# Reordering the opening of a one-core hybrid mLSTM and MoE layer: q in passes by kind of product, gate rows at full precision, one modulation chunk by TensorE

## What is computed

```python
shift_a, scale_a, gate_a, shift_f, scale_f, gate_f = silu(c) @ w_ada + b_ada     # 6 x 1024, for two conditions
h = rmsnorm(x, g_pre_mix) * (1.0 + scale_a) + shift_a
z = h @ w_in                        # u 512, q 512, k 512, v 512, o 512, gate_pre 16 columns
y_pool = pool_mixer(u, w_pool, pool_scale, grid)
y_ml, C, n, m = mlstm_mixer(q, k, v, o, gate_pre, b_gate, C0, n0, m0)    # two directions, 4 heads of 128
x = x + gate_a * rmsnorm(concat([y_pool, y_ml]) @ w_out, g_post_mix)
h = rmsnorm(x, g_pre_ffn) * (1.0 + scale_f) + shift_f
x = x + gate_f * rmsnorm(moe(h), g_post_ffn)    # 64 experts, top 6 in 4 of 8 groups, and a shared expert
```

## Time and profile before

| | us |
|---|---|
| median of 3 runs | 728.69 (728.23 to 728.75) |
| the profiled execution, its own time | 728.3 |
| its span, first to last instruction | 726.2 |
| mean granted TensorE clock | 0.99 of full speed |

### The profile page before, as it was taken

How to read it: one execution, slowest core, us unless ns; L and a number is a source line. 1 busy time by engine, 2 the same in 40 slices (tenths; PEclk the granted TensorE clock), 3 DMA queues, 4 the chain that set the end, 5 groups by cost and what they waited for, 6 DMA issues and landing times.

```text
span 726.2 us, 11392 instructions
## 1 busy us (share of the span) xinstructions
PE 683.2 (94%) x4205; PEld 396.8 (55%) x4205; DVE 391.9 (54%) x1003; ACT 192.0 (26%) x329; POOL 89.0 (12%) x53
## 2 busy tenths in 40 slices
PE   1789999998999999999999999999999999998993
PEld 1689888777865645544444544454445445444431
DVE  3488999695298444454444444454445437442115
ACT  3244334474272311211111111111111121130113
POOL 2445544422303000000000000000000000000000
PEclk9999999999999999999999999999999999999997
DMA  9999866625579569999999999999999999999994
GB/s 321 374 351 336 260 232 232 246 103 165 155 286 423 248 251 416 427 423 427 399 383 426 426 427 423 421 424 424 425 426 423 428 422 427 424 425 424 419 409 192
DMA packets 51012, 259.14 MB, mean 357 GB/s; under 512 B 6704, under 2 KB 9312, under 8 KB 32904
## 3 DMA queue, kind: packets, MB, share of 16 engines
q1 hardware_dynamic: 46816, 252.50, 86.2%
q0 software_dynamic: 1584, 4.90, 2.0%
q10 hardware_dynamic: 2552, 0.98, 0.5%
HBM read 254.64 MB, written 3.71 MB: 356 GB/s over the span
## 4 chain that ended last, share of the span: by engine, by line
PE 80%; DMA 8%; SPq 4%; DVE 4%; issue 2%; ACT 1%; POOL 0%; DVEq 0%; ACTq 0%
PE psum L2414 23%; PE psum L2422 11%; PE psum L2302 10%; PE psum L2386 9%; PE psum L600 5%; PE psum L601 5%; PE psum L602 5%; DMA w_gu<-in_w_expert_gu 4%; PE psum L2263 3%; DMA w_gu<-in_w_ada 2%; DMA w_dn<-in_w_expert_down 2%; PE psum L2314 2%; SPq L796 1%; PE psum L2373 1%; PE psum L2006 1%
## 5 line engine op out<-in xcount | busy, mean ns | idle before, releaser
L2414 PE MATMUL psum<-w_gu,hgT 128*32 128x512 f32 (+1 forms) x1280 | 191.4, 594 | 2.1 <-DMA w_gu<-in_w_expert_gu 2.1
L2414 PEld LDWEIGHTS psum<-w_gu,hgT 128*32 128x32 f32 (+1 forms) x1280 | 57.3, 119 | 127.8 <-issue 127.6
L1781 DVE TENSOR_TENSOR f_acc<-f_acc,psum 128x512 f32<-128x512 f32 x132 | 86.7, 684 | 43.3 <-PE psum L2386 43.3
L2422 PE MATMUL psum<-w_dn,actT 128*32 128x512 f32 (+1 forms) x640 | 98.7, 597 | 1.4 <-DMA w_dn<-in_w_expert_down 0.9
L1759 DVE SCALAR_TENSOR_TENSOR act<-sil,wsl,psum 128x256 f32<-128x256 f32 x27 | 18.4, 682 | 127.8 <-ACT sil L1115 118.5
L585 POOL TENSOR_TENSOR w_lo<-w_gu,w_hi 128x2048 fp32r<-128x2048 f32 x13 | 59.8, 4597 | 75.4 <-ACT w_hi L876 75.4
L2302 PE MATMUL psum<-onehot,h_lo 128*128 128x512 f32 (+1 forms) x168 | 66.7, 397 | 0.0
L2302 PE MATMUL psum<-onehot,h_hi 128*128 128x512 f32 (+1 forms) x168 | 65.3, 389 | 0.0
L1765 DVE TENSOR_TENSOR y_lo<-psum,y_hi 128x1024 fp32r<-128x1024 f32 x26 | 31.8, 1224 | 51.0 <-ACT y_hi L1119 51.0
L2422 PEld LDWEIGHTS psum<-w_dn,actT 128*32 128x32 f32 (+1 forms) x640 | 27.0, 119 | 58.5 <-issue 57.8
L1115 ACT ACTIVATE sil<-psum 128x256 f32<-128x256 f32 x27 | 10.4, 384 | 173.2 <-PE psum L2414 173.2
(11 more groups left out here) (322 smaller groups left out, 861.4 us busy)
## 6 DMA issues: line engine op xcount, KB each, us to landing
w_gu<-in_w_expert_gu SPq DMA_DIRECT2D x49, 2048.0 KB, 17.5
w_dn<-in_w_expert_down SPq DMA_DIRECT2D x61, 1024.0 KB, 14.9
w_gu<-in_w_expert_gu SPq DMA_DIRECT2D x27, 1024.0 KB, 16.0
w_gu<-in_w_ada SPq DMA_DIRECT2D x12, 2048.0 KB, 13.9
w_gu<-in_w_in SPq DMA_DIRECT2D x4, 2048.0 KB, 12.9
w_gu<-in_w_out SPq DMA_DIRECT2D x2, 2048.0 KB, 9.2
bc<-mod_rows POOLq DMA_DIRECT2D x6, 512.0 KB, 7.3
w_gu<-in_w_expert_gu SPq DMA_DIRECT2D x6, 512.0 KB, 20.4
```

The costliest lines, as they stand in the source:

```text
L1781: v.tensor_tensor(dst, dst, bank(5 + n), ALU.add).then_inc(f_added, 1)
L2414: ins = t.matmul(bank(target)[rows, :], column(c)[:, rows], w_gu[s][:, c, :], start=(c == 0), stop=(c == NC - 1), tile_position=(0, rows.s ...
L2422: ins = t.matmul(bank(target + n)[rows, :], actT[:, j, rows], w_dn[s][:, j, 512 * n:512 * (n + 1)], start=(j == 0), stop=(j == 1), tile_po ...
```

## The change

- **Start.** ACT takes the table of Sqrt first, squares x, and only then makes silu(c). TensorE transposes x before ada(0). Products whose result nobody reads (`keep_warm`, 128 x 512 at full precision) stand before (1) and after (3) modulation_T(0).
- **q.** z_chunk("q") becomes q_chunk: by half and by kind of product. Of the first half, the high products of heads 0 to 2, then ada(1), the w_hi x tT_lo products, ada(3), the w_lo products, with modulation_T(1) among them, and then head 3. Of the second half, all high products, all w_hi x tT_lo, all w_lo.
- **Gates.** No split. wgs holds 32 columns (16 of them zero), and each of the 12 products (four of hT for the last four row blocks, four of tT_hi and four of tT_lo for the first four) is made at full precision in one of four column tiles, into bank 3. The first four (`gates_second`) come after q's first half, the rest (`gates_first`) right behind. ACT copies bank 3 to gate_part; a product with gate_sum, made of ident on DVE, adds the four tiles into bank 6 (`gates`). tT_lo of the last four row blocks, which overwrites hT, now waits for gates_second.
- **a4.** Is multiplied directly by TensorE (ada(4)) after q, and loaded behind k instead of ahead of it. DVE's sums and the total of a4 are gone.
- **Order.** DVE's gate chain comes right after tT_lo; sums of a5 come after g_nat. ACT's Exp and Ln come after two heads of q, the w_hi of k's second half after all four, and the w_hi of v's first half after k's first half and the Exp of the scans. TensorE's gate transposition (`gates_T`) stands between the halves of v.

```diff
-            issued = ["a0", "a2", "q", "a1", "a3", "q", "a4", "k", "v", "a5", "a6", "o", "a7"] + order[chunk["u"]:]
+            issued = ["a0", "a2", "q", "a1", "a3", "q", "k", "a4", "v", "a5", "a6", "o", "a7"] + order[chunk["u"]:]
...
             high(2)
-            for n in range(4):
-                z_evac(n)
-            high(3)
+            z_evac(0)
+            z_evac(1)
             a.wait_ge(abs_ready, 1)
             own.link(a.activation(g_t[:, :], g_t[:, :], ACT.Exp, scale=-1.0))
             a.activation(g_t[:, :], g_t[:, :], ACT.Ln, bias=1.0).then_inc(soft_ready, 1)
-            high(4)
-            for n in range(4, 8):
-                z_evac(n)
-            high(5)
+            z_evac(2)
+            z_evac(3)
+            high(3)
...
+            high(4)
+            for n in range(4, 8):
+                z_evac(n)
+            high(5)
             high(6)
...
             def low_tokens(n):
                 first, end = PARTS[n]
                 v.wait_ge(th_ready, n + 1)
+                if first >= 4:
+                    v.wait_ge(gates_done, 1)
...
-            ada_sums(4)
-
-            v.wait_ge(gates_done, 1)
+            v.wait_ge(gates_done, 3)
...
             v.tensor_tensor(g_b[:, :], g_b[:, :], g_mx[:, :], ALU.add).then_inc(scans_ready, 1)
-            ada_sums(5)
+            ada_evac(4)
             v.wait_ge(scans_ready, 1)
...
+            ada_sums(5)
             ada_sums(6, 0, 5)
-            ada_evac(4)
...
-            ada(0)
             t.wait_ge(const_in, 16)
...
+            ada(0)
             ada(2)
...
+            def gate_parts(last, operands):
+
+                for c, token_part in operands:
+                    j = c % 4
+                    ins = t.matmul(bank(3, 0, T)[32 * j:32 * j + 32, :], wgs[:, c, :], token_part,
+                                   start=(c >= 4), stop=(last and token_part is operands[-4 + j][1]), tile_position=(0, 32 * j))
+                ins.then_inc(gates_done, 1)
...
+            def q_chunk():
+
+                q_high((0, 1, 2), 0)
+                ada(1)
+                q_high_low((0, 1, 2), 0)
+                ada(3)
+                q_low((0, 1), 0)
+                modulation_T(1)
+                q_low((2,), 0)
+                t.wait_ge(mod_ready, 4)
+                q_high((3,), 0)
+                q_high_low((3,), 0)
+                q_low((3,), 0).then_inc(half_used, 1)
+                gates_second()
+                gates_first()
+                q_high(range(H), 1)
+                gates()
+                q_high_low(range(H), 1)
+                q_low(range(H), 1)
...
                     if half == 0:
                         ins.then_inc(half_used, 1)
+                        if w == "v":
+                            gates_T()
```

More of the change, by code:

```diff
@@ L859, in _ @@
             a.dma_start(const[:, :], t_in["shape_constants"]).then_inc(const_in, 16)
-            a.wait_ge(ct_in, 32)
-            a.activation(scT[:, :, 0:2], ct.rearrange("p m c -> p c m"), ACT.Silu).then_inc(sc_ready, 1)
+            own.link(a.activation(sum_sq2[:, 0:1], eps, ACT.Sqrt))
             a.wait_ge(x_in, 16 * NT)
@@ L866, in _ @@
             a.activation(sum_sq, sum_sq, ACT.Sqrt, bias=eps, scale=1.0 / D).then_inc(sq_ready, 1)
+            a.wait_ge(ct_in, 32)
+            a.activation(scT[:, :, 0:2], ct.rearrange("p m c -> p c m"), ACT.Silu).then_inc(sc_ready, 1)
             def high(k):
@@ L953, in _ @@
             high(10)
[L954 removed]
+            a.wait_ge(ada_summed, 3)
             for n in range(14, 17):
@@ L1222, in _ @@
                 v.memset(sel[:, m, m:m + 1], 1.0).then_inc(sel_ready, 1)
-            own.add(v.memset(wg_hi[:, :, :].bitcast(F32), 0.0))
-            own.add(v.memset(wg_lo[:, :, :].bitcast(F32), 0.0))
+            v.memset(wgs[:, :, :], 0.0).then_inc(zeroed, 1)
+            own.add(v.memset(gate_sum[:, :], 0.0))
             own.add(v.memset(v1[:, :, :, DH:DV], 1.0))
@@ L1231, in _ @@
                 v.tensor_scalar(xn[:, i, :], x[:, i, :], rstd[:, i:i + 1], None, ALU.mult).then_inc(xn_ready, 1)
+            v.wait_ge(const_in, 16)
+            own.link(v.tensor_reduce(gate_row[:, :], ident.rearrange("p (j r) -> p r j", j=4), AX.X, ALU.add))
+            for d in range(2):
+                v.tensor_copy(gate_sum[:, :].rearrange("p (g d r) -> p g d r", g=2, d=2)[:, :, d, 0:H],
+                              gate_row[:, 8 * d:8 * d + 8].rearrange("p (g h) -> p g h", g=2)).then_inc(sel_ready, 1)
             def ada_evac(i):
@@ L1241, in ada_evac @@
                 wait_chunk(v, f"a{max(i, 2 + i % 2)}")
-                b = 6 + i % 2
-                v.tensor_tensor(modrow[:, i, :], bank(b, P * (i % 4), P * (i % 4) + P), modrow[:, i, :], ALU.add)\
+                v.tensor_tensor(modrow[:, i, :], ada_direct(i), modrow[:, i, :], ALU.add)\
                     .then_inc(mod_ready, 1)
@@ L2014, in ada_total @@
                 t.wait_ge(sel_ready, 2)
-                t.wait_ge(mod_ready, i if i == 4 else min(i - 1, 7))
+                t.wait_ge(mod_ready, min(i - 1, 7))
                 t.wait_ge(z_act, 8)
@@ L2031, in _, with keep_warm @@
                     ins = t.transpose(psum[:, T * c + P * i:T * c + P * i + P], xn[:, i, P * c:P * c + P], ident)
+            ada(0)
             ada(2)
+            def keep_warm(n):
+                for _ in range(n):
+                    t.matmul(bank(7), xn[:, 0, 0:P], xn[:, 0, 0:512], start=True, stop=True)
+            keep_warm(1)
             def modulation_T(half):
@@ L2043, in _, with q_part @@
             modulation_T(0)
-            ada(1)
+            keep_warm(3)
+            WI_TI, WI_TL, WL_TI = range(3)
+            def q_part(h, half, product, js):
+                s = chunk["q"] % PSLOTS
+                cols = slice(DH * h, DH * (h + 1))
+                for j in js:
+                    c = 4 * half + j
+                    w = w_lo[s][:, c, cols] if product == WL_TI else w_hi[half][:, j, cols]
+                    x_part = tT_lo[:, c, :] if product == WI_TL else tT_hi[half][:, j, :]
+                    ins = t.matmul(bank(z_bank(h), 0, T), w, x_part, start=(c == 0 and product == WI_TI),
+                                   stop=(c == NC - 1 and product == WL_TI))
+                return ins
@@ new lines, in q_high, with q_high_low @@
+            def q_high(heads, half):
+                t.wait_ge(w_hi_ready, half + 1)
+                for n, js in enumerate(((0, 1), (2, 3))):
+                    t.wait_ge(th_ready, 2 * half + 2 if half == 0 else 2 * half + n + 1)
+                    for h in heads:
+                        q_part(h, half, WI_TI, js)
+            def q_high_low(heads, half):
+                for n, js in enumerate(((0, 1), (2, 3))):
+                    t.wait_ge(tl_ready, 2 * half + n + 1)
+                    for h in heads:
+                        q_part(h, half, WI_TL, js)
@@ new lines, in q_low @@
+            def q_low(heads, half):
+                t.wait_ge(w_lo_ready, half + 1)
+                for h in heads:
+                    ins = q_part(h, half, WL_TI, range(4))
+                    if half:
+                        ins.then_inc(gu_used[chunk["q"] % PSLOTS] if h == H - 1 else z_done, 1)
+                return ins
+            def gate_parts(last, operands):
[4 more added lines that the diff above has]
+                ins.then_inc(gates_done, 1)
@@ new lines, in gates_second, with gates_first, gates @@
+            def gates_second():
+                t.wait_ge(gate_in, 16 * 5)
+                t.wait_ge(h1_dve, 2 * (NC - len(ON_ACT)))
+                t.wait_ge(h1_act, 2 * len(ON_ACT))
+                gate_parts(False, [(c, hT[:, c, :]) for c in range(4, NC)])
+            def gates_first():
+                gate_parts(True, [(c, tT_hi[0][:, c, :].bitcast(F32)) for c in range(4)]
+                           + [(c, tT_lo[:, c, :].bitcast(F32)) for c in range(4)])
+            def gates():
+                t.wait_ge(gate_part_ready, 1)
+                t.wait_ge(sel_ready, 4)
+                t.wait_ge(modT_ready, 2)
+                t.matmul(bank(6, 0, T), gate_sum[:, :], gate_part[:, :], start=True, stop=True).then_inc(gates_done, 1)
@@ L2068, in z_chunk @@
                             c = 4 * half + j
-                            if n == 0 and j == 2:
-                                t.wait_ge(tl_ready, 2 * half + 2)
-                            if w in "qk":
+                            if w == "k":
                                 cols = slice(DH * i, DH * (i + 1))
@@ L2082, in z_chunk, with gates_T @@
                         ins.then_inc(half_used, 1)
+                        if w == "v":
+                            gates_T()
+            def gates_T():
+                t.wait_ge(w_ready, 2)
+                t.wait_ge(nat_ready, 9)
+                for a_ in range(3):
+                    for tile in range(NT):
+                        col = T + 24 * a_ + 8 * tile
```

(12 more changed lines are left out.)

51 lines of the change are left out of this document (25 added, 26 removed).

## The result

The changed kernel takes 736.57 us (median of 4 runs, 735.84 to 737.14) against 728.72 for the kernel before: ratio 1.0108, 95% interval 1.009 to 1.0125. It is 7.85 us slower. The forecast was 2.2 us faster, and the time lies 8.3 us above the upper end of its range. The profiled execution took 737.14 us, the longest of the four, with a span of 735.0, 8.8 more than before.

The account below looks back on a forecast made before the run. TensorE was taken as the bound, VectorE 1.3 us from it. a9's total 3.45 us earlier, less 1.2 for the clock, gave net -2.2: 726.5 us median (726.1 for the profiled execution), range 724.0 to 728.3.

Parts of the forecast that it names:

- Up to 36.7 nothing, 24 products of q done: Start: reordering hidden behind chunks a1 and a3, no time won, but 24 of q's 96 products done by 36.7 instead of 12.
- Gates: After q's first half: gate passes in four column tiles take 2.2 us, closing sum 0.7, replacing 24 products of 4.2 us.
- Rival 4: Gate passes at 384 columns do not run side by side: 8.7 us instead of 2.2, total 731.2; chance 0.07.
- a4 directly, k earlier: After q: 11 us of VectorE sums go, TensorE pays 1.95 instead of 1.27; k starts at 55.05 instead of 58.46.
- w_hi of v's first half, "wanted at 72.0, there at 71.7": Ahead of v: ScalarE's w_hi 65.1 to 67.0 behind the scans, GpSimd done at 71.7, TensorE wanting it at 72.0.
- my upper bound of 64.9: Gate chain: latest end of VectorE's scans, all blocked by GpSimd's w_lo from 58.6; 60.1 without blocking, 64.2 taken.
- rival 2: Clock falls at gate transposition, or k's w_hi a microsecond late: v ends 1 to 1.8 later, -1.0, 727.7; chance 0.17.
- a9's total at 129.3: End of u: VectorE's last v copy at 91.8 plus 37.4 us of work puts a9's total at 129.3 instead of 132.75.
- What follows a9's total: Behind a9's total: only a clock cost was counted, 1.2 us; no wait for the copy.
- The restart of the clock, 1.2 us: After TensorE's wait before a9's total: slow clock costs 1.2 us, between bounds of nothing and 1.8.
- VectorE, not TensorE, last at a9's total: At a9's total: TensorE is through u at 125.5 and waits for VectorE until 129.3.
- The expert stage keeps its length: Expert stage: TensorE and DMA both at their limit, length unchanged, so time saved in the opening is kept.

Follow-up runs that it names:

- version with all four repairs: Changed kernel with early ident_r copy, three unread products ahead of a9's total, gate transposition in three parts, w_hi of v's first half ahead of ScalarE's DMA issues: 727.04 us.
- the filling: Three unread products ahead of a9's total: 728.78 us on top of the early ident_r copy (732.47 without); alone, with three more behind the total, 731.79 against the change's 736.57.
- the filled version: Changed kernel with the ident_r copy made at the start and three unread products ahead of a9's total: 728.78 us.

## Why the prediction was wrong, point by point

The profiled span is 11.0 us above the forecast (735.0 for 724.0). By the table of landmarks, 4.0 of them are there at a9's total (the late v), 3.2 come at the copy behind it, 3.6 from the slow clock beyond the 1.2 that were allowed, and 0.3 later. The two steps that failed most: the copy behind a9's total, whose wait the sum put at nothing, and the restart of the clock, which it put at 1.2 us and which took 4.8.

- **Up to 36.7 nothing, 24 products of q done.** Right. ada(3) began at 34.61, against 34.73.
- **Gates.** Right in size: from the first of the 24 instructions (42.15) to q's next product (44.53) are 2.4 us, and in the version with all four repairs 2.1 (42.35 to 44.43), against 2.2 in the sum. So four column tiles run side by side at 384 columns too. The Trainium skill (TensorE: Matmul & The Clock Gate, "Measured speedup vs the span model") gives 3.07 times for four row tiles; the 2.8 us estimated from it for these column tiles is more than either took. Rival 4, the only one that ended on the slower side, was wrong in its mechanism.
- **a4 directly, k earlier.** Right: 1.95 us on TensorE, k at 55.59 for 55.05. That VectorE's sums were worth taking away was not tested by itself.
- **w_hi of v's first half, "wanted at 72.0, there at 71.7".** Wrong by 2.5 us, two terms of the sum. I let one scan slip in ahead of GpSimd and took 64.2 for the end of the scans; the scan came 0.01 us too late and took 5.16 us [after: 59.23], so it was 65.4. That is above my upper bound of 64.9. And I let ScalarE's w_hi follow the Exps. It moved past four DMA issues on ScalarE's own queue, whose price I had not counted (1.44 us). With 0.3 us of cover, 1.7 came through to v.
- **Clock at the gate transposition.** Named as rival 2 and left out of the sum. It fell in the profiled execution (clock 0.92 over v, 1.8 us) and in some executions of the experiments.
- **a9's total at 129.3.** 133.27. VectorE's 37.4 us behind v's last copy were exact (95.56 to 132.96), so this is the late v and nothing else. v ended 4.15 us late: k 0.5, w_lo 1.7, clock and transposition 1.9.
- **What follows a9's total.** This step was missing. The prediction asked which VectorE operations would newly meet a w_lo, and asked it of the gate chain and of g_nat, where work was moved. It did not ask it of the seam where both engines arrive at another time though nothing of it was edited. TensorE got ahead of VectorE by 2.75 us. GpSimd's last w_lo follows TensorE (w_hi waits for u's end), the copy follows VectorE, so w_lo came in front of the copy. Before, w_lo (134.53) was 1.7 us behind it. By the forecast's own numbers w_lo would have run from about 128 to 132.6 and the copy would have stood at 129.4: the same rule that priced the gate chain would have shown it. Measured: 3.9 us for the copy, and 3.0 to 4.1 us of the whole.
- **The restart of the clock, 1.2 us.** Mechanism right, size wrong by four times: 4.8 us by the landmarks, 3.7 to 4.8 by the filling. The nearest row was the wait ahead of a1. The 0.84 read there is a mean over five microseconds. By the table by microsecond (one line of it below) the clock stood at 0.50 from about 28.4 to 31.9, and was back within 3 us of the first work (29.29). That work was ada(1), 64 instructions in four column tiles. Here TensorE went on with maxima of four rows and the small products of the pooling, and stayed at 1.2 GHz for ten busy microseconds. What a fallen clock costs was not the same behind the two waits. That the kind of work decides it is my reading; no run changed the work alone.
- **VectorE, not TensorE, last at a9's total.** Right, and this was the trouble: the gain on TensorE was larger than that on VectorE, and the difference was paid as a wait.
- **The expert stage keeps its length.** Right within 0.3 us.

From the kernel before, behind the wait ahead of a1 (PE busy, clock, DMA share, GB/s):

```profile
30.00:31.00 1.00, 1.00 (x24) 0.50 1.05 387
```

The Trainium skill (SBUF — State Buffer, "SBUF: two separate sides") has VectorE and GpSimd take a shared pair of ports as an exclusive lock. This case agrees: the copy took 3.92 us beside w_lo and 0.17 without it, and the scan, an operation with two SBUF inputs, 5.16 and 0.72. The rule had been read correctly and applied in too few places.

What stays open: how often the clock falls behind the block of the gate transposition and around a9's total, and whether the filling of the start is worth 1.0 us, since its trace accounts for 0.3.

## What to carry to other kernels

When one engine gets ahead of another, list every operation that follows the first and every one that follows the second at the next seam, edited or not, and look for pairs whose order turns round; a copy of 0.17 us cost 3 to 4 here. Constants belong at the start, not at a seam. Where a change makes TensorE wait for the first time, do not price the clock from a mean over a stretch: read how long it stays low, and what work comes behind the wait. And fill the wait with unread products if that work is on the path: here it gave back 3.7 to 4.8 us.

## What was not expected of the hardware

A granted clock of 0.50 held for 13.6 us, ten of them with TensorE busy in every microsecond (137 to 147), on work of 4 x 384 and 128 x 256 operands. The same work ran at 1.00 throughout in the kernel before and in the filled version. So it did not lower a high clock in any execution profiled here, and it left a low one low for ten microseconds.
